# Moving the two halves of the retention output's split behind the last softmax window

## The reference

```
h = rmsnorm(x, g_mix)
z = h @ w_in          # 1024 x 5888: attention q, k, v; retention q, k, v; rg, ga, gb
ya = sliding_window_sink_attention(rope(aq), rope(ak), av, sinks) @ w_a
r = chunkwise_retention(rot(rq), rot(rk), rv)
r = r * rsqrt(mean(r*r) + EPS) * silu(rg)
yb = r @ w_b          # 1024 x 1024
x = x + (sigmoid(ga) * ya + sigmoid(gb) * yb) @ w_out
h2 = rmsnorm(x, g_mlp)
x = x + square(relu(h2 @ w_up)) @ w_down
```

## Time and profile before

| | us |
|---|---|
| median of 3 executions | 1009.11 |
| profiled execution | 1008.58 |
| its span, first to last instruction | 1006.8 |
| PE busy | 999.8 |
| PEld busy (weight loads, beside PE) | 846.1 |
| DVE busy | 726.5 |
| ACT busy | 501.8 |
| POOL busy | 170.3 |

### The profile page before, as it was taken

The page is one execution under the profiler, slowest core; times in us unless marked ns, Lnnn a source line. Parts: engine busy times, 40 slices in busy tenths (PEclk is TensorE's granted clock), DMA queues, the critical chain, the costliest instruction groups (busy, mean ns, idle before and its releaser), DMA issues.

```text
span 1006.8 us, 13509 instructions
## 1 busy us (share of the span) xinstructions
PE 999.8 (99%) x5621; PEld 846.1 (84%) x5621; DVE 726.5 (72%) x805; ACT 501.8 (50%) x610; POOL 170.3 (17%) x129
## 2 busy tenths in 40 slices
PE   9999999999999999999999999999999999999997
PEld 7888787888888888888877888888887899899796
DVE  5885785766665656785785767788877767789974
ACT  6544553455444436444564355444468555644352
POOL 0520000000000000430000020000000149169730
PEclk9999999999999999999999999999999999999999
DMA  9796665555555454597574457556544754355451
GB/s 347 247 297 239 190 187 173 190 182 173 203 186 190 167 195 161 188 297 243 183 218 164 164 165 269 179 177 213 196 167 140 246 168 168 125 168 152 111 188 42
DMA packets 106396, 192.80 MB, mean 191 GB/s; under 512 B 9352, under 2 KB 20704, under 8 KB 106208
## 3 DMA queue, kind: packets, MB, share of 16 engines
q1 hardware_dynamic: 106160, 191.85, 58.1%
q10 hardware_dynamic: 176, 0.09, 0.0%
HBM read 182.79 MB, written 6.82 MB: 188 GB/s over the span
## 4 chain that ended last, share of the span: by engine, by line
PE 99%; DVE 0%; ACT 0%; issue 0%; DVEq 0%; ACTq 0%
PE bank L816 13%; PE bank L818 12%; PE bank L819 12%; PE bank L1121 11%; PE bank L841 10%; PE bank L845 9%; PE bank L852 9%; PE bank L1125 6%; PE bank L1203 2%; PE bank L1430 1%; PE bank L998 1%; PE bank L1014 1%; PE bank L1417 1%; PE bank L850 1%; PE bank L843 1%; PE bank L1106 1%
## 5 line engine op out<-in xcount | busy, mean ns | idle before, releaser
L1911 DVE TENSOR_TENSOR w_lo<-arena,w_hi 128x2048 fp32r<-128x2048 f32 (+1 forms) x80 | 185.0, 2323 | 97.7 <-ACT w_hi L1518 97.3
L1911 DVE TENSOR_TENSOR w_lo<-raw,w_hi 128x2048 fp32r<-128x2048 f32 (+1 forms) x78 | 180.7, 2327 | 80.2 <-ACT w_hi L1518 79.9
L1518 ACT ACTIVATE w_hi<-raw 128x2048 fp32r<-128x2048 f32 (+1 forms) x83 | 157.1, 1893 | 104.9 <-PE bank L819 72.9
L1518 ACT ACTIVATE w_hi<-arena 128x2048 fp32r<-128x2048 f32 (+1 forms) x80 | 151.3, 1892 | 106.0 <-PE bank L819 82.2
L1121 PE MATMUL bank<-hT,w_hi 128*128 128x512 f32 x504 | 123.4, 391 | 0.0
L2539 POOL TENSOR_TENSOR rstd<-mean,const 128x1 f32<-128x1 f32 (+1 forms) x16 | 9.1, 578 | 632.2 <-DVE mean L1920 462.8
L1121 PEld LDWEIGHTS bank<-hT,w_hi 128*128 128x128 f32 x504 | 92.3, 188 | 17.5
L816 PE MATMUL bank<-w_hi,hT 128*128 128x512 f32 (+1 forms) x248 | 95.3, 384 | 0.0
L819 PE MATMUL bank<-w_hi,hT 128*128 128x512 f32 (+1 forms) x224 | 85.5, 382 | 0.0
L818 PE MATMUL bank<-w_lo,hT 128*128 128x512 f32 (+1 forms) x224 | 85.5, 382 | 0.0
L816 PE MATMUL bank<-w_hi,uT_hi 128*128 128x512 f32 x208 | 81.2, 390 | 0.0
(11 more groups left out here) (356 smaller groups left out, 1915.4 us busy)
## 6 DMA issues: line engine op xcount, KB each, us to landing
arena<-in_w_in SPq DMA_DIRECT2D x22, 1024.0 KB, 5.4
raw<-in_w_in SPq DMA_DIRECT2D x20, 1024.0 KB, 6.0
arena<-in_w_up SPq DMA_DIRECT2D x16, 1024.0 KB, 5.6
raw<-in_w_up SPq DMA_DIRECT2D x16, 1024.0 KB, 5.2
arena<-in_w_down SPq DMA_DIRECT2D x16, 1024.0 KB, 5.1
raw<-in_w_down SPq DMA_DIRECT2D x16, 1024.0 KB, 5.3
raw<-in_e_w_in SPq DMA_DIRECT2D x6, 1024.0 KB, 5.2
arena<-in_e_w_in SPq DMA_DIRECT2D x6, 1024.0 KB, 5.4
```

The costliest lines, as they stand in the source:

```text
L1518: act.activation(w_hi[:, p % SPLIT_RING, :, 0:n], raw_at(p)[:, :, 0:n], copy).then_inc(hi_ready, 1)
L1911: dve.tensor_tensor(w_lo[:, s, :, 0:n], raw_at(p)[:, :, 0:n], w_hi[:, s, :, 0:n].bitcast(F32), ALU.subtract).then_inc(lo_ready, 1)
```

## The change

On ScalarE, in group g = 11, the uT_hi activation stands behind `window(l, 10)` and no longer ahead of it. On VectorE, the uT_lo subtraction no longer lies inside the softmax of window 10; it stands behind the loop over the groups, after the split of the loop's last step (piece 25) and ahead of `window(l, 11)`. The other use of `between`, a small mean at g = 7, stays.

```diff
                 for g in range(W_IN_GROUPS):
                     if l or g:
                         step(p + 2 * g)
+                    window(l, g - 1)
                     if g == W_IN_GROUPS - 1:
                         act.wait_ge(r_turned, l + 1)
                         act.activation(uT_hi[:, :, :], r_rows, copy).then_inc(r_hi, 1)
-                    window(l, g - 1)
                     if g != RQ:
                         step(p + 2 * g + 1)
                     group_out(l, g)
...
-            def beside_exp(l, g):
-
-                if g == 7:
-                    retention_mean(l, 1)
-                if g == W_IN_GROUPS - 2:
-                    dve.wait_ge(r_hi, l + 1)
-                    dve.tensor_tensor(uT_lo[:, :, :], r_rows, uT_hi[:, :, :].bitcast(F32), ALU.subtract).then_inc(r_lo, 1)
...
-                    softmax(l, g - SCORES_AT, between=lambda: beside_exp(l, g))
+                    softmax(l, g - SCORES_AT, between=(lambda: retention_mean(l, 1)) if g == 7 else lambda: None)
...
+                dve.wait_ge(r_hi, l + 1)
+                dve.tensor_tensor(uT_lo[:, :, :], r_rows, uT_hi[:, :, :].bitcast(F32), ALU.subtract).then_inc(r_lo, 1)
                 window(l, W_IN_GROUPS - 1)
```

## The result

The changed kernel takes 1020.38 us (median of 5 executions, 1019.76 to 1021.77), against 1009.17 us before (5 executions): a ratio of 1.0112, with a 95% interval from 1.0098 to 1.0128. It is slower, as forecast, but by 11.2 us where 7.3 us were forecast. That is 1.4 us above 1019.0, the upper end of the range for 8 in 10.

What follows compares the result with a forecast made beforehand. TensorE, busy 999.8 of 1006.8 us, was taken as the bound. Two stalls of 3.77 us, 7.54 us, on 1008.58 or 1009.11 gave 1016.12 or 1016.65; forecast 1016.4 us, range for 8 in 10 1014.0 to 1019.0.

Steps and rivals of the forecast that it cites:

- all the steps on the queues: Layer 0 starts after the move: uT_hi 147.43, w_hi 149.26, w_lo 151.20, uT_lo 153.41 us; TensorE stalls 3.77 us per layer.
- the four followers that I called hidden: ScalarE's last evacuations, VectorE's next copy and o_lo, w_lo of piece 26, and piece 29's refill come later without reaching TensorE.
- first rival: Later TensorE waits shrink and give back some of the stall, at most 2.4 us: 1014.0 us; chance 0.07.
- third: Not slower: ScalarE's early copies end the exponentials 3.77 us sooner, uT_lo is ready in time, 1009 us; chance 0.04.
- fourth: A weight piece is late as well, by a long subtraction or late slot: stalls reach 6.0 us, 1020.9 us; chance 0.04.
- The clock: TensorE's granted clock stays full through each 3.77 us stall, as in the kernel's tail; nothing added to the sum.
- The prediction's own signs of being wrong: uT_lo ends before TensorE arrives, a gap under 3 or over 4.5 us, or span growth unequal to the two gaps.
- The second rival: TensorE runs at half clock for 4.2 us behind each stall, losing 2.1 us twice: 1020.6 us; chance 0.11.
- the upper bound of a stall: TensorE's stall per layer with a handover as long as the longest single earlier wait, 0.3 us: 4.02 us.

Runs made afterwards that it cites:

- the full-clock run: The changed kernel plus 15 calls of useless 128-column matmuls on TensorE ahead of each wait for uT_lo: 1016.3 us, ratio 1.0069.
- VectorE's half alone: The changed kernel with uT_hi back in its old place on ScalarE, so only uT_lo is moved: 1014.7 us, ratio 1.0054.
- behind a filler: The changed kernel plus 7 calls of useless 128-column matmuls on TensorE at the head of each stall: 1017.77 us, ratio 1.0083.
- by 26: The changed kernel plus 26 calls of useless 128-column matmuls on TensorE ahead of each wait for uT_lo: 1020.41 us, ratio 1.0109.

## Why the prediction was wrong

Right were all the steps on the queues. uT_hi, w_hi, w_lo and uT_lo start within 0.15 us of the computed times; the stalls are 3.67 and 3.66 us long where 3.77 was forecast for each; the four followers that I called hidden are hidden, as the full-clock run shows (1016.3 us against the sum of 1016.1 to 1016.65). Nothing was given back later (first rival), the early copies brought nothing forward (third), no piece was late (fourth).

The step that failed is *The clock*: "an idle stretch of 4.3 us was borne at full clock here, and I count 3.77 us as borne too". It put the clock at nothing in the sum; measured were 2.72 us in layer 0 and 1.54 us in layer 1, 4.26 us together, and the filler of 15 calls took them away with both stalls left in place. The prediction's own signs of being wrong show it as well: the span grew by 11.9 us and not by the 7.3 us of the two gaps, TensorE was busy 4.6 us longer, and the matmuls behind the gap came 0.43 us apart. The tail of the kernel before was one draw. In the changed kernel's own tail the clock fell about 2.2 us after the last matmul, and in VectorE's half alone it fell behind a gap of 2.1 us in one layer and not in the other. So one idle stretch that passed at full clock doesn't show that the next one will. The second rival, to which I gave 0.11, was what happened. Its price of 1020.6 us came out close (1020.38) by luck: it took half of 4.2 us, so 2.1 us for each stall, where 2.72 and 1.54 us were measured, and the two errors cancel. The first stretch of the kernel from which it took the 4.2 us is odd besides. Its records start 0.23 us apart, half the pace of the 0.112 us at full clock, but the clock column says 1.00 there, and nothing here shows why:

```profile
2.00:4.00 2.00, 2.00 (x12) 2.00 (x11) 0.00 (x0) 0.92 (x1) 0.00 (x0) 1.00 0.92 313
```

In "TensorE: Matmul & The Clock Gate" of the Trainium skill, the section "HAM oscillation — how this bites in real kernels" tells of a matmul stream cut by waits that starts at half clock behind each of them. Layer 0 of this trace agrees: 155.85 to 161.8 at 0.50. Layer 1 agrees only in part, since its first 0.9 us behind the gap ran at 1.00. The evidence that I set against the section was a single row of another place.

One bound was misread as well, without effect on the outcome: the longest single wait behind the earlier trace rows is 0.4 us and not 0.3, so the upper bound of a stall would have been 4.12 us.

What stays open is what decides whether the clock falls at a given gap. In the profiled executions it fell behind one of the two gaps of 2.1 us, one of the two of 2.0 us (behind a filler), both of 2.8 us and all three of 3.8 us, once in the gap and otherwise 0.4 to 1.2 us after the restart. The gaps filled by 15 calls, 0.23 us idle, and by 26 had no fall in either layer.

## What to carry to other kernels

A step taken out of a wait of its engine and put behind an instruction that waits for something later inherits that wait: find what is queued ahead of it, follow that to its releaser, and compare the end with the time at which the bounding engine asks. Where the bounding engine is TensorE, price a new gap at its length plus a fall of the clock: behind gaps of 2.0 to 3.8 us a fall cost 1.4 to 2.7 us here where it came, and only the shortest gaps (2.0 and 2.1 us) sometimes had none. Other matmuls in the gap took that part away. Order took away all of it: the late operand first on its own engine, or last among the products.

## What the runs showed of the hardware

The clock can fall after TensorE is at work again: 0.9 us after the restart in layer 1 of the changed kernel, 1.2 us in the run with the change in layer 0 alone. It fell behind idle gaps of 2.1 us in one of two cases and behind 3.8 us in three of three. At 0.50 a 128-column weight load took 0.33 us instead of 0.19, and a pair of load and 512-column matmul came every 0.43 us instead of every 0.23. A float32 matmul of 128 columns is two records of 0.112 us each (52 in 5.83 us).
